# GpSimd's low halves of the routes' up tiles, written as four subtractions of 256 columns in place of one of 1024

## The reference, cut to what matters

```python
def peer_ffn(h, w_q, sub_keys, u_tab, v_tab):
    ...
    q = (hf @ w_q).astype(f32).reshape(t, PEER_HEADS, 2, PEER_HALF_DIM)
    s = jnp.einsum('thjd,jnd->thjn', q, sub_keys.astype(f32))
    sv, si = lax.top_k(s, PEER_TOPK)
    comb = (sv[:, :, 0, :, None] + sv[:, :, 1, None, :]).reshape(t, PEER_HEADS, PEER_TOPK * PEER_TOPK)
    cand = (si[:, :, 0, :, None] * PEER_N_KEYS + si[:, :, 1, None, :]).reshape(t, PEER_HEADS, PEER_TOPK * PEER_TOPK)
    best, pick = lax.top_k(comb, PEER_TOPK)
    experts = jnp.take_along_axis(cand, pick, axis=-1)
    gates = jax.nn.softmax(best, axis=-1)
    ...
        act = jax.nn.gelu(jnp.einsum('td,thkd->thk', hb, u_tab[eb]).astype(f32), approximate=False)
        return jnp.einsum('thk,thkd->td', (gb * act).astype(hb.dtype), v_tab[eb])
```

## Time and profile before

| | us |
|---|---|
| median of three runs | 2312.95 (2312.63 to 2314.08) |
| the profiled execution | 2312.89, span 2311.1 |
| TensorE busy with matmuls | 2227.0 (96%) |
| VectorE busy | 1755.5 (76%) |
| ScalarE busy | 1122.6 (49%) |
| GpSimd busy | 1050.8 (45%) |
| GpSimd's low halves (L736, 179 of them) | 456.0, mean 2.548 each |
| of these, the 43 of the change | start at 1065.1 to 1270.8, median 2.409 each |

### The profile page before, as it was taken

One profiled execution on the slowest core, in us unless ns is written; L12 is line 12 of the kernel. 1 busy time (PEld: TensorE's weight loads), 2 busy tenths in 40 slices (PEclk: granted clock), 3 DMA queues, 4 the chain that ended last, 5 costly groups with the idle time before them and its releaser, 6 DMA issues.

```text
span 2311.1 us, 43747 instructions
## 1 busy us (share of the span) xinstructions
PE 2227.0 (96%) x14976; PEld 2150.3 (93%) x14976; DVE 1755.5 (76%) x3436; ACT 1122.6 (49%) x2154; POOL 1050.8 (45%) x604
## 2 busy tenths in 40 slices
PE   7999889999999999999999999999999999999997
PEld 7999769999889999999999999999999999999996
DVE  8985685445648325888999988888578989899996
ACT  6554784456652213433434877878333333333332
POOL 3333365445444433344656544444534444544442
PEclk9999999999999999999999999999999999999998
DMA  3322345433125323234445899999999999999994
GB/s 129 116 83 81 127 154 201 157 124 116 59 73 155 103 86 127 93 127 146 145 143 202 294 328 330 334 336 359 375 369 394 393 386 393 389 388 383 384 385 146
DMA packets 225642, 526.50 MB, mean 228 GB/s; under 512 B 23792, under 2 KB 117072, under 8 KB 225376
## 3 DMA queue, kind: packets, MB, share of 16 engines
q1 hardware_dynamic: 144384, 284.47, 35.4%
q0 software_dynamic: 46240, 167.89, 19.8%
q10 hardware_dynamic: 34912, 72.78, 8.5%
HBM read 453.44 MB, written 72.80 MB: 228 GB/s over the span
## 4 chain that ended last, share of the span: by engine, by line
PE 64%; issue 17%; ACT 8%; POOL 6%; ACTq 2%; DVE 1%; DMA 1%; POOLq 0%; SPq 0%; DVEq 0%
PE ps L1473 24%; PE ps L877 17%; PE ps L1342 8%; POOL wlo L736 5%; PE ps L1058 4%; PE ps L1097 3%; ACT rinv L2041 2%; ACT whi L1568 2%; ACT g_block L2066 1%; ACT onehot_i L2045 1%; PE ps L1041 1%; PE ps L1428 1%; PE ps L1235 1%; ACT tmp L1983 1%; PE ps L1204 1%
## 5 line engine op out<-in xcount | busy, mean ns | idle before, releaser
L736 POOL TENSOR_TENSOR wlo<-raw,whi 128x1024 fp32r<-128x1024 f32 x179 | 456.0, 2548 | 597.9 <-ACT whi L1568 597.8
L1568 ACT ACTIVATE whi<-raw 128x1024 fp32r<-128x1024 f32 x373 | 394.1, 1057 | 675.7 <-PE ps L1473 214.3
L1342 PE MATMUL ps<-h_hi,whi 128*128 128x416 f32 x1008 | 359.8, 357 | 17.7 <-DVE wlo L2879 10.7
L748 POOL DMA_INDIRECT row<-pu,row_idx x160 | 230.1, 1438 | 291.6 <-DVE row L2870 213.6
L1473 PE MATMUL ps<-act_hi,whi 128*128 128x416 f32 x1000 | 351.1, 351 | 3.4 <-DVE act_lo L2941 3.4
L1342 PE MATMUL ps<-h_lo,whi 128*128 128x416 f32 x1008 | 353.3, 351 | 0.0
L1342 PE MATMUL ps<-h_hi,wlo 128*128 128x416 f32 x1008 | 353.2, 350 | 0.0
L1473 PE MATMUL ps<-act_lo,whi 128*128 128x416 f32 x1000 | 351.1, 351 | 0.0
L1473 PE MATMUL ps<-act_hi,wlo 128*128 128x416 f32 x1000 | 350.9, 351 | 0.0
L748 POOL DMA_INDIRECT row<-pv,row_idx x160 | 232.3, 1452 | 245.4 <-DVE row_acc L2928 177.8
L2879 DVE TENSOR_TENSOR wlo<-raw,whi 128x1024 fp32r<-128x1024 f32 x194 | 236.9, 1221 | 90.5 <-ACT whi L1568 89.5
(11 more groups left out here) (410 smaller groups left out, 4731.1 us busy)
## 6 DMA issues: line engine op xcount, KB each, us to landing
raw<-wt SPq DMA_DIRECT2D x245, 512.0 KB, 3.5
raw<-pv SPq DMA_DIRECT2D x128, 512.0 KB, 9.4
activations<-tmp ACTq DMA_DIRECT2D x128, 208.0 KB, 4.2
gates_dense<-g_block ACTq DMA_DIRECT2D x52, 512.0 KB, 6.7
g_tiles<-gates_dense SPq DMA_DIRECT2D x32, 832.0 KB, 9.3
gelu<-activations SPq DMA_DIRECT2D x128, 208.0 KB, 10.7
a_cum_rows<-decay_sums SPq DMA_DIRECT2D x32, 256.0 KB, 3.3
state_s<-s_in SPq DMA_DIRECT2D x16, 512.0 KB, 7.6
```

Source lines behind the costliest of these rows:

```text
L736: pool.tensor_tensor(lo, raw[n.par][:, :], hi.bitcast(F32), ALU.subtract).then_inc(split_ready, 1)
L748: pool.indirect_dma_start(GR[b][:, :], None, table[:, :], bass.IndirectOffsetOnAxis(ap=IDX[:, s:s + 1], axis=0))\
L1342: mm = pe.matmul(PS[2 * p.par][:, 0:DT], w[slot][:, k, :], x[:, k, 0:DT], start=k == 0 and w is whi and x is HH, stop=k == KD - 1 and w is ...
L1568: act.activation(whi[slot][:, :, :].rearrange("p k c -> p (k c)"), raw[n.par if n.b < N_V else slot][:, :], ACT.Copy)\
```

## The change

GpSimd's low halves of tiles 134 to 176 are written by a new function: four subtractions of 256 columns, of which the last raises the semaphore. The loop is cut at tile 134; what comes before it stays as it was. The outputs are the same numbers.

```diff
+            def low_pieces(n):
+
+                slot = slot_of(n)
+                pool.wait_ge(hi_done, n.v + 1)
+                for q in range(4):
+                    hi, lo = [w[slot][:, 2 * q:2 * q + 2, :].rearrange("p k c -> p (k c)") for w in (whi, wlo)]
+                    ins = pool.tensor_tensor(lo, raw[n.par][:, 2 * q * P:(2 * q + 2) * P], hi.bitcast(F32), ALU.subtract)
+                ins.then_inc(split_ready, 1)
+
...
-            with pool.Fori((N_PQ + 5) // 2, N_GU // 2 - 4) as i:
+            with pool.Fori((N_PQ + 5) // 2, N_ROUTE // 2) as i:
                 for k in range(2):
                     low(Idx(k, i, 2))
+            with pool.Fori(N_ROUTE // 2, N_GU // 2 - 4) as i:
+                for k in range(2):
+                    low_pieces(Idx(k, i, 2))
             pool.wait_ge(picks_ready, 1)
             for k in range(11):
-                low(Idx(N_GU - 9 + k))
+                low_pieces(Idx(N_GU - 9 + k))
                 if k % 2 == 0:
                     rows(k // 2)
```

## The result

The changed kernel took 2324.5 us (median of five runs, 2323.2 to 2327.5), the kernel before 2313.4 beside it (2312.6 to 2314.2): a ratio of 1.005, 95% interval 1.0035 to 1.0065. It is slower by about 11 us. The forecast was 2322.9, range 2313 to 2334. The profiled execution has a span of 2321.4 us, 10.3 more than before, at a mean granted clock of 0.994 against 0.993.

The account below looks back on a forecast made before the run. TensorE, its matmuls filling 96% of the span, was taken as the bound. New waits of 20.4 us, less 10 for old waits and 0.4 at the gate turn, gave +10 on 2312.9: 2322.9 us, range 2313 to 2334.

Parts of the forecast that it names:

- Price of a piece: On GpSimd, one 256-column subtraction was to take 0.77 us, or 0.61 after its release if it had waited.
- A low half that meets nothing costs nothing: On GpSimd, an undisturbed low half in four pieces grows by 0.6 us, below the slack of 0.78.
- VectorE gets in between two pieces that stand back to back: On GpSimd's pieces: VectorE takes turns between them; multiply near 1.7 us, add near 1.2; chance 0.67.
- The first meeting: Low half meeting the one-hot chain at its head: takes 6.35 us in place of 4.50; TensorE's tile loses 3.2.
- The pace of the chain: VectorE's one-hot half chain shrinks from 9.7 to about 6.4 us, so its second comparison meets the next low half.
- What goes: TensorE's nine old waits for GpSimd and two for VectorE's route parts vanish, giving back 10 us.
- pieces that hold together: Rival on GpSimd: VectorE gets in only behind the fourth piece and falls behind; about +15 us, 2328; chance 0.10.
- Little changes: Rival at the one-hots: pieces near 0.6 us, one tile a chunk loses; 10 to 14 lost against 10; chance 0.16.
- Faster: Rival at the one-hots: every comparison falls between two low halves, all 10 us of loss go, 2303; chance 0.07.
- who VectorE waits for: After the first two chunks, VectorE, some 6 us a chunk faster, waits for TensorE's turned parts at L2759.
- the distance in the locked chunks: Last three chunks: comparison 1.3 us ahead of a low half, losing 1.9 then 1.8, 3.7 us each.
- no clock drop: On TensorE after long waits: no clock drop in the forecast; up to five, 0 to +8 us, in the range.

Follow-up runs that it names:

- e1_quiet: Changed kernel with only the six low halves before the first one-hot chain cut in four, the other 37 whole; ratio 1.0003 to the kernel before.
- e5: Kernel before, low halves whole, with VectorE's one-hot comparison written as four of 512 columns; ratio 0.9996 to the kernel before.
- e7: Kernel before with low halves in two pieces and VectorE's comparison in four; ratio 0.9980, on another chip 0.9986, to the kernel before.
- e4_half: Changed kernel without the second one-hot half chain of each chunk, its result copied from the first; 2322.0 us, ratio 1.0040 to the kernel before.
- e2_two: Changed kernel with low halves in two pieces of 512 columns in place of four; 2317.2 us, ratio 1.0012 to the kernel before.
- e3_eight: Changed kernel with low halves in eight pieces of 128 columns in place of four; 2347.9 us, ratio 1.0151 to the kernel before.

## Why the prediction was right, and where it was not

**Right, with its numbers.** *Price of a piece*: 0.74 measured, 0.77 taken (0.60 against 0.61 after its release, by the two rows of step 2 below); L781's 0.62 was the worse neighbour. *A low half that meets nothing costs nothing*: e1_quiet shows it. *VectorE gets in between two pieces that stand back to back*: multiply and add at 1.64 and 1.10 on the mean (1.7 and 1.2 predicted), reduce 1.22. Behind this, the Trainium skill, page "SBUF — State Buffer", section "Who interferes with whom", has it that issue order decides who blocks. The trace agrees in the first meeting, where the comparison issued 0.13 us ahead; what it adds is that between two pieces it is VectorE, which had waited, that goes, and not the GpSimd instruction that stands next. *The first meeting*: low half from 1095.64 to about 1101.9, 6.2 us against 6.35; TensorE's loss 1101.93 - 1098.63 - 0.19 = 3.1 against 3.2. *The pace of the chain*: a half chain of 6.4 us against 6.4, so two low halves a chunk are hit. *What goes*: both waits for parts.

The rivals: pieces that hold together would have left the multiply at 3.3 or more, it is 1.65. "Little changes" needed one hit a chunk or pieces near 0.6: there are nine waits at meetings and pieces of 0.74. (The forecast of the profile said fewer waits than the old nine, which did not fit its own two hits a chunk.) "Faster" needed comparisons that fall between low halves: none of the five chunks did so in the changed kernel.

**The sum, term by term.** Predicted +10 = 20.4 lost - 10 (old waits) - 0.4 (at the gate turn). Measured in the stretch +13.0: 21.5 idle, 3.2 slow, and 11.7 given up of what was there before (6.5 + 1.5 + 3.7 of turn). The idle term was 1.1 too small, the slow term, which I had at nothing, is 3.2 (half of it the clock drop of step 3, the rest some 0.1 behind each wait and turning), and the gain was 1.3 larger than predicted: 10 + 1.1 + 3.2 - 1.3 = 13.0. The span then had -2.7 from stretches of identical code, which makes 10.3. That the span's difference is so near the forecast owes something to this; the medians, +11.1, are the sounder measure.

**Wrong step 1: who VectorE waits for.** The walk had VectorE wait for its turned parts (then L2759) from the third chunk on. It waits somewhere else. VectorE's waits, and one of them beside ScalarE's rows:

```profile
DVE gate_sum L2839 <- ACT expert_parts L2036: 30.0, 4, 11.2
...
1151.80 0.29 DVE L2839 TENSOR_REDUCE gate_sum<-expert_parts 128x8 f32<-128x128 f32 x1 [11.16 <-ACT expert_parts L2036]
1148.23 1.06 ACT L1580 ACTIVATE whi<-raw 128x1024 fp32r<-128x1024 f32 x1 [3.06 <-PE ps L1354]
1151.39 0.31 ACT L2036 ACTIVATE expert_parts<-expert_parts 128x128 f32<-128x128 f32 x1
```

ScalarE's exponential of the picks stands in ScalarE's queue behind high halves that keep TensorE's pace. VectorE, ready early, waits there for 30.0 us in four places, at the end of the second to fifth route; the waits for turned parts are 0.26 to 0.47 each but for 13.7 at the last. The slack that the change makes on VectorE ends there, and is worth nothing beyond the two waits at the turning. That VectorE is held to TensorE's pace from the third chunk on was as predicted, for another reason.

**Wrong step 2: the distance in the locked chunks.** I put the comparison 1.3 us ahead of a low half in each of the last three chunks, and expected 1.9 + 1.8 lost. In the third it stands 0.27 us behind the low half's first piece, in the last two 0.74 and 0.67 ahead. The fourth chunk:

```profile
1204.28 2.29 DVE L2828 TENSOR_TENSOR onehot_pick<-pick_parts_f,pick_steps 128x2048 bf16<-128x2048 bf16 x1
1205.02 2.15 POOL L744 TENSOR_TENSOR wlo<-raw,whi 128x256 fp32r<-128x256 f32 x1 [1.91 <-ACT whi L1580]
```

The first piece takes 2.15 and TensorE waits 2.44 + 1.53 us in this chunk, 2.50 + 1.57 in the next; the first two (comparison 0.13 ahead and 0.12 behind) have 2.95 + 1.46 and 2.98 + 1.05 and the third one wait of 3.24. So the later the comparison stands against the low half, the longer the first wait and, where there is one, the shorter the second. By chunk the idle time is 4.7, 4.4, 3.4, 4.3 and 4.4 us, where 4.9, 4.4 and three times 3.7 were predicted: that the sum of 20.4 came so near rests in part on luck, as the last two chunks lose more than predicted and the third less.

**Wrong step 3: no clock drop.** I took none in the forecast and up to five in the range. There was one, behind the longest wait (the last two rows have the columns of the earlier trace rows):

```profile
1174.38 0.45 PE L1354 MATMUL ps<-h_hi,whi 128*128 128x416 f32 x1 [3.24 <-POOL wlo L744]
...
1176.10 0.55 PE L1354 MATMUL ps<-h_hi,wlo 128*128 128x416 f32 x1
...
1176.00:1180.00 4.00, 4.00 (x14) 3.86 (x14) 3.93 (x3) 0.00 (x0) 4.00 (x2) 0.59 0.29 113
1180.00:1184.00 4.00, 4.00 (x23) 3.98 (x23) 1.82 (x2) 2.52 (x3) 2.05 (x4) 1.00 0.52 184
```

The granted clock reads 0.59 in the four us from 1176, matmuls are 0.35 apart in place of 0.19, and 14 ran where 23 do: about 1.7 us. This chunk has no second wait. That the slowed tile, which took longer, let the next low half come in time, so that the drop cost less than its length, is argued and not shown.

**Not seen in advance**, and without weight here: VectorE's short integer instructions on the picks wait for pieces too. The same kind of instruction, held up and free:

```profile
1091.93 0.76 DVE L2817 TENSOR_SCALAR pick_parts<-pick 128x128 uint32<-128x128 uint32 x1
1094.19 0.23 DVE L2820 TENSOR_SCALAR pick_parts<-pick_parts 128x128 uint32<-128x128 uint32 x1
```

The page of the Trainium skill cited above says that tensor_scalar instructions can contend for the shared pair. The kernel before shows it too, whole low halves and all: its L2808, the second of these two instructions, took 0.23 us in two chunks and 2.30 and 2.40 in two others. I had not gone over these rows.

## What to carry to other kernels

Where two engines share a resource for whole instructions, a cut on one side is a turn for the other. So the first to cut is the longest instruction of the engine that is *not* waited for, and the one that the bound engine waits for stays whole, or nearly so. That alone gave nothing here (e5, 0.9996), as the other engine became the late one; the only gain, 0.2% or less, came with one cut on the side that is waited for (e7). So look at the waits on both sides after each cut.

Busy time that falls on an engine says nothing until one has followed what it waits for next. Here 27 us went to an engine whose queue ended at another's. And when a change brings new waits of 2 to 3 us on TensorE, give the clock a term in the sum, not only in the range: here such waits brought it down in one kernel and not in another.

## What the runs showed of the hardware that was not expected

*The clock after a wait is not decided by the wait's length alone.* In the changed kernel waits of 2.44, 2.50, 2.95 and 2.98 us passed without a drop and 3.24 brought one. In e4_half waits of 2.94, 3.27 and 2.50 us each brought one (0.57, 0.58 and 0.61 granted over the four us shown) and 2.45 did not; in e2_two 2.50 and 2.29 did. The matmuls are then 0.35 us apart in place of 0.19, the clock at its lower level. After 5.3 us (e3_eight) it read 0.50, and 0.50 at the end of the 7.6 of e5_cmp4 and behind it. What tells the 2.50 and 2.95 of the one kernel from the 2.50 and 2.94 of the others no run here shows; the question stays open.

*What a subtraction costs by its size on GpSimd*, met by nothing: 0.46 us for 128 columns, 0.74 for 256, 1.30 for 512, 2.40 for 1024. That is (2.40 - 0.46) / 896 = 2.17 ns a column and 0.18 us fixed: the pieces themselves are cheaper than I took them, and what is let in between is what costs.

*Profiles of the same code differ by some us before and behind the stretch* (the start of the stretch 1050.5 to 1056.6), so that a change of 3 us can be read from the stretch but not from one span.
